# A hybrid decoder layer: order of copies, joins, chunks and the triangular solve in its front stage

## The chip, the cores and the metric

One NeuronCore of a Trainium2 chip runs the whole layer as one program. The metric is the device time of one execution in microseconds. The engines are TensorE (PE), VectorE (DVE), ScalarE (ACT), GpSimd (POOL) and SyncE (SP), which here issues the DMAs. Each engine runs its own list of instructions in order; semaphores make one wait for another.

## The reference, cut to what matters

For x of 1024 positions by 1024 columns: `h = RMSNorm(x)`; one projection `h @ w_in` gives an HGRN2 group (q, f, i, gate; four heads of 128) and a gated DeltaNet group (q, k, v through a causal convolution of width 4 with silu, z, and two gates per head).

```python
f = lb + (1.0 - lb) * jax.nn.sigmoid(hf)
o_a = hgrn2_chunked(silu(hq), 1.0 - f, hi, log(f))           # cumulative sum of log f in each chunk
qkv = silu(causal_dwconv(gqkv, gdn_conv)); gq, gk = l2_normalize(...)
system = eye + strict_lower((k * beta) @ k.T * exp(g_t - g_s)) # per chunk and head: its inverse is needed
attn = (q @ k.T) * exp(g_t - g_s)
```

Both groups are scanned over the chunks, gated, sent through `w_out` and added to x; then come a convolution-gated MLP (2816 wide) and a small embedding part. All of it is float32, with matmul operands split in a high part and a remainder (three matmuls for one product).

## The kernel before, in words

The order of work is written out by hand in `Front` (one method per engine). The kernel uses chunks of 128 positions, eight of them (NT = 8).

*Split products.* A weight slab is loaded into `w_raw`, rounded by ACT into `w_whi` (`Slabs.round`, L167; pieces L358), and DVE computes the remainder `w_wlo` (`Slabs.remainder`, L182; pieces L365). PE then does three matmuls for each of them.

*Conv pairs.* The 12 tiles of the DeltaNet q, k, v (128 columns each) are made in 6 pairs, each by seven products of half size in the Winograd form of Strassen's method: B21, T2, T3, T1, (B11 of the next pair), B22, T4, in `Pieces.order`. B11, T2, T1 and B22 of a pair accumulate one after the other in one PSUM bank, and between them ACT copies the bank out (`act_pair_copy`, L1060); PE opens the bank again only when that copy is done. DVE joins copies and banks into the convolution line (`dve_pair_join`, L1458), ACT copies B22 to the line (`act_pair_line`, L1072) and does the first tap (L1088), DVE the other three (`dve_taps`, L1468), ACT the silu (L1093). For the eight tiles of q and k come squares (ACT L1104, L1116; DVE remainder L1475) and a small matmul that sums them (`pe_sum`, L950). POOL forms the sums of weight blocks (L328 to L339). At the last pair ACT and DVE compute the decay factors (`act_factors`, `dve_factors`).

*Chunks and f units.* PE then computes eight units of f (head and half, `F_UNITS`), each 24 matmuls (L936 to L938), in 16 slots of 12. Between them it does the chunks: `pe_chunk` (transposed spreads L788, scores L793) in the second half of slot `SPREAD[c]` and `pe_chunk_turn` (transposes, L802) in the first half of the next. For each chunk DVE shifts (L1632), ACT takes exponentials (L1291, L1294) and scales the keys (L1299), DVE does four products (L1640 to L1649), and SP stores the tiles lt, at and kd (`sp_chunk`, L607). ACT applies the sigmoid to a finished f unit (L1242); each change between Sigmoid, Exp, Ln and Silu loads a table (ACT_TABLE_LOAD). `dve_open` (L1618, L1620) turns the sigmoid into f and 1 − f, `act_log` (L1283) takes the logarithm, `dve_cumulate` (L1610) the running sum, called a scan of f below.

*Solve.* Blocks of 32 × 32 of the stored lt are loaded back (`b_blk`), DVE inverts them in 31 steps of two operations (`dve_solve`, L1672, L1675), with slab remainders at given steps; POOL cuts x and its transpose xt out of it (L680, L683), SP stores them and loads them in scan form. Meanwhile PE does the f units and then eight units of q; in these lie the four steps of the first chunk's inverse (`INVERSE_AFTER`, L1861). Then the scan over the chunks starts (ACT L2045, L1272, L2036; DVE L2189), and later the output projection, the MLP and the embedding part.

SP's queue around the change is: reload of `saved`, per chunk the three stores with slab loads after chunks 1, 2 and 5, the blocks, lt, two slabs, then x stored, waited for and loaded, xt stored, waited for and loaded.

Of the kernel before, what the change touches and what calls it, by code (L numbers as in the profile page):

```python
# [54 lines left out]
class Kit:  # L55


    def __init__(self, nc, ctx):
        self.nc, self.ctx = nc, ctx
        self.psum = ctx.enter_context(nc.psum_tensor("psum", [P, 8, BANK], F32))  # L60
        c = lambda name, shape: ctx.enter_context(nc.sbuf_tensor(name, shape, F32))
        self.ident = c("ident", [P, P])
        self.ones = c("ones", [P, P])
        self.tri = c("tri", [P, P])
        self.future = c("future", [P, P])
        self.cols = c("cols", [P, N_COLS])
        self.eps = c("eps", [P, 2])
        self.lb = c("lb", [P, 2 * NH])

        self.spare = c("spare", [P, 2])  # L70
        with ExitStack() as early:
            w = lambda name: early.enter_context(nc.sbuf_tensor(name, [P, DM], F32R))
            self.more_hi, self.more_lo = ([w(f"w_more_{n}{u}") for u in range(2)] for n in ("hi", "lo"))
        with ExitStack() as rows:
            r = lambda name: rows.enter_context(nc.sbuf_tensor(name, [P, NH, BANK], F32))
            self.row_copy1, self.row_copy = r("row_copy1"), r("row_copy")
        with ExitStack() as pairs:
            r = lambda name, shape: pairs.enter_context(nc.sbuf_tensor(name, shape, F32))
            self.pair_line = [r(f"gconv_line{u}", [P, GK - 1 + SEQ]) for u in range(2)]
            self.pair_sum, self.pair_raw = r("pair_sum", [P, BANK]), r("pair_raw", [P, DM])  # L80
            self.gate_z = r("gate_z", [P, 10, NT, NH])
        with ExitStack() as blocks:
            r = lambda name, shape: blocks.enter_context(nc.sbuf_tensor(name, shape, F32))
            self.blk, self.xo, self.xto = (r("b_" + n, [P, SB, SB]) for n in ("blk", "x", "xt"))
            self.tmp = r("b_tmp", [P, SB * SB // 4])
        with ExitStack() as chunks:
            r = lambda name, shape: chunks.enter_context(nc.sbuf_tensor(name, shape, F32))
            r("a_more_before", [P, 2, SB, SB])
            self.more_lt, self.more_at = r("a_more_lt", [P, DG]), r("a_more_at", [P, DG])
        self.ed = [c(f"s_h_ed{i}", [P, DG]) for i in range(3)]  # L90
# [280 lines left out]
class Front:  # L371
# [6 lines left out]
    SPREAD = tuple(range(NT))  # L378
# [4 lines left out]
    INVERSE_AFTER = ((2, 1, 0), (3, 0, 0), (3, 0, 1), (3, 1, 1))  # L383
# [4 lines left out]
    def __init__(self, nc, k, a, shared, heads_on, rows_out, scratch, saved):  # L388
# [20 lines left out]
        with ExitStack() as chunks:  # L409
            self.dec = [s(f"a_dec{i}", [P, DG], c=chunks) for i in range(2)]  # L410
            self.egb, lt, at, self.kd = (s("a_" + n, [P, DG], c=chunks) for n in ("egb", "lt", "at", "kd"))
        self.lt, self.at = (lt, k.more_lt), (at, k.more_at)
# [26 lines left out]
        with ExitStack() as projecting:  # L439
# [5 lines left out]
        names = ("made", "loaded", "kept", "soft", "picked", "wrow", "squared", "rooted", "inverted", "scaled", "rounded_x",  # L445
                 "begun", "tapped", "freed", "smooth", "sq", "sq_hi", "sq_lo", "gate_in", "gate_hi", "gate_lo", "act", "dve",
                 "gated", "bounded", "logged", "summed", "ready", "shifted", "decayed", "queried", "lt_stored", "at_stored",
                 "kd_stored", "zeroed", "blocks", "solved", "cut", "x_stored", "opened", "formed", "sum_rounded", "sum_rest",
# [23 lines left out]
    def sp(self, sp):  # L472
# [68 lines left out]
        sp.wait_ge(s["lt_stored"], NT * 16)  # L541
# [10 lines left out]
        for n, (name, src) in enumerate((("x", self.xo), ("xt", self.xto))):  # L552
            sp.wait_ge(s["cut"], n + 1)
            for b in range(P // SB):
                at = slice(b * SB, (b + 1) * SB)
                sp.dma_start(self.scratch[name][at, :, at].rearrange("i g j -> g i j"), src[at, :, :]).then_inc(s["x_stored"], 16)
            sp.wait_ge(s["x_stored"], (n + 1) * (P // SB) * 16)
            self.scan.load_part(sp, name, 0, (self.scan.x, self.scan.xt[0])[n])
        for i in range(self.STAGES):
            sp.wait_ge(self.stored[i], 6 * 16)  # L560
        for name in ("at", "kd"):
            sp.wait_ge(s[name + "_stored"], NT * 16)
        for j in range(2):
            self.slabs.load(sp, first["q"] + NH + 1 + j)

# [37 lines left out]
    def sp_chunk(self, sp, c):  # L603
        part = slice(c * NH, (c + 1) * NH)
        for name, key, tile in (("lt", "a_kk", self.lt[c % 2]), ("at", "a_qk", self.at[c % 2]), ("kd", "a_k", self.kd)):
            self.banks.released(sp, (key, c))
            sp.dma_start(self.scratch[name][:, part, :], heads(tile[:])).then_inc(self.s[name + "_stored"], 16)  # L607
# [59 lines left out]
    def pool(self, pool):  # L667
# [14 lines left out]
        pool.wait_ge(s["at_stored"], NT * 16)  # L682
# [259 lines left out]
    def pe_sum(self, pe, m):  # L942
        at = self.place(m)
        pe.wait_ge(self.s["sq_lo"], at + 1)
        if at == 0:
            pe.wait_ge(self.s["picked"], 1)
# [171 lines left out]
    def act(self, act):  # L1118
# [35 lines left out]
        act.activation(self.pick[:], self.ones8[:], ACT.Copy).then_inc(s["picked"], 1)  # L1154
# [32 lines left out]
        for i, (p, q) in enumerate(pc.order):  # L1187
# [44 lines left out]
        for slot in range(self.SLOTS):  # L1232
# [3 lines left out]
            if slot == NT:  # L1236
                self.act_log(act, (0, 1))
            if slot % 2:
# [3 lines left out]
                self.banks.release(act.activation(self.f[:, h, half * BANK:(half + 1) * BANK], self.banks.of(key), ACT.Sigmoid), key)  # L1242
# [4 lines left out]
        self.act_log(act, (2, 3))  # L1247
        for name in ("lt", "at", "kd"):
            act.wait_ge(s[name + "_stored"], NT * 16)
        act.wait_ge(s["queried"], NT)  # L1250
        for h in range(NH - 1):
            for half in range(2):
# [3 lines left out]
                if half == 1:  # L1256
                    slabs.round(act, first["q"] + h + 2, m_)
        act.wait_ge(pc.made, pc.sums_made() + 1)
# [26 lines left out]
    def act_slot(self, act, slot):  # L1285
        s, small = self.s, self.small
        for c in range(NT):
            if self.SPREAD[c] == slot:
# [7 lines left out]
                if c:  # L1296
                    act.wait_ge(s["kd_stored"], c * 16)
                for h in range(NH):
                    ins = act.activation(heads(self.kd[:])[:, h, :], self.banks.of(("a_k", c))[:, h * P:(h + 1) * P], ACT.Copy,  # L1299
# [20 lines left out]
    def act_factors(self, act):  # L1320
        s, z, small, k = self.s, self.z, self.small, self.k
# [6 lines left out]
        act.sem_inc(s["act"], 1)  # L1328
        act.activation(z[:, 9], self.lnr[:, :, NH:2 * NH], ACT.Exp, scale=-0.5).then_inc(s["act"], 1)
# [5 lines left out]
        k.table(act, ACT.Silu)  # L1335
# [124 lines left out]
    def dve_taps(self, dve, m):  # L1460
        s, line, acc, at = self.s, self.line[m % 2], self.qkv[:, m, :], self.place(m)
        for q in range(1, GK):
            if q == 1:
                dve.wait_ge(s["begun"], at + 1)
            else:
                dve.wait_ge(s["tapped"], 2 * at + q - 1)
            tap = self.k.cols[:, C_GCONV + q * 3 * NH + m:C_GCONV + q * 3 * NH + m + 1]
# [9 lines left out]
    def dve(self, dve):  # L1477
# [68 lines left out]
        for i, (p, q) in enumerate(pc.order):  # L1546
# [29 lines left out]
            elif q == pc.T4:  # L1576
                self.dve_taps(dve, 2 * p + 1)
        self.dve_pair_join(dve, last, pc.T4)
        slabs.remainder(dve, self.first["f"] + 1)
        self.dve_taps(dve, 2 * last)  # L1580
        first = self.first
        for slot in range(NT):
            self.dve_slot(dve, slot)
            if slot in (5, 7):
                self.dve_open(dve, (slot - 5) // 2)
                slabs.remainder(dve, first["f"] + self.ROUNDED_AT[slot])
            if slot == 3:
                dve.memset(self.keep, 1.0).then_inc(s["ready"], 1)
                dve.wait_ge(s["ready"], 1)
                dve.memset(self.keep.rearrange("p (c t) -> p c t", t=P)[:, :, 0:1], 0.0).then_inc(s["ready"], 1)  # L1590
# [7 lines left out]
        dve.wait_ge(s["x_stored"], 2 * (P // SB) * 16)  # L1598
# [7 lines left out]
    def dve_cumulate(self, dve, h):  # L1606
        s = self.s
        dve.wait_ge(s["ready"], 2)
# [3 lines left out]
    def dve_open(self, dve, h):  # L1612

        s, k, f, kk = self.s, self.k, self.f[:, h, :], self.kk[:, h, :]
        for half in range(2):
            self.banks.released(dve, ("f", h, half))
        dve.wait_ge(s["kept"], 7)
# [4 lines left out]
    def dve_slot(self, dve, slot):  # L1622
        s, small, future = self.s, self.small, self.k.future
        for c in range(NT):
            if self.SPREAD[c] == slot:
# [11 lines left out]
                if c > 1:  # L1637
                    dve.wait_ge(s["lt_stored"], (c - 1) * 16)
                    dve.wait_ge(s["at_stored"], (c - 1) * 16)
# [11 lines left out]
    def dve_solve(self, dve):  # L1651
# [5 lines left out]
        for i in range(SB - 1):  # L1657
            if i == 9:
                slabs.remainder(dve, first["q"])
            elif i == 11:  # L1660
                self.dve_open(dve, 2)
            elif i == 17:
                self.dve_open(dve, 3)
# [76 lines left out]
class Scan:  # L1740
# [533 lines left out]
    def dve(self, dve):  # L2274
        s = self.s
        dve.wait_ge(self.front.s["summed"], NH)
        dve.wait_ge(self.front.s["x_stored"], 2 * (P // SB) * 16)
# [75 lines left out]
    def pool(self, pool):  # L2353
        pool.wait_ge(self.front.s["x_stored"], 2 * (P // SB) * 16)
# [1668 lines left out]
```

## Time and profile before

| | us |
|---|---|
| median of three runs | 1448.48 (1447.63 to 1450.18) |
| the profiled execution | 1446.5 |
| its span, first to last instruction | 1444.8 |
| PE busy | 1399.9 |
| DVE busy | 1098.4 |
| ACT busy | 753.7 |
| POOL busy | 287.2 |

The profile is of one execution. Busy shares are averages over stages; the windows split them, and the granted clock tells at which of its two levels (1.2 and 2.4 GHz) PE ran: 1.00 is always the upper one.

### The profile page before, as it was taken

What the parts mean: (1) busy time and instruction counts of PE and PEld (TensorE: products, weight loads), DVE (VectorE), ACT (ScalarE), POOL (GpSimd) and SP (SyncE); (2) the same over time, 40 slices, a digit from 0 to 9 for tenths busy, and PEclk for the clock granted to TensorE, in tenths of its full rate; (3) what the DMA queues carried; (4) which work ended last, traced back from release to release, by engine and by line L of the source; (5) the groups of instructions that cost most, each with busy time, mean ns of one, the idle gap of its engine ahead of it and who ended that gap; (6) DMA issues with size and microseconds to landing.
All of it is one profiled execution on the core that took longest, in us unless ns stands there. A gap on an engine that the chain in (4) does not pass through costs nothing.

```text
span 1444.8 us, 19770 instructions
## 1 busy us (share of the span) xinstructions
PE 1399.9 (97%) x7067; PEld 1171.0 (81%) x7067; DVE 1098.4 (76%) x1598; ACT 753.7 (52%) x1369; POOL 287.2 (20%) x279
## 2 busy tenths in 40 slices
PE   9999989877999999999999999999999999999998
PEld 7788866667788999888888888888888888888886
DVE  7843577755757988357997999999999686577567
ACT  6444455754437888347673434344444544454455
POOL 3251321111027877010000000000000154400000
PEclk9999999998999999999999999999999999999999
DMA  9715232245434333545442234335326765424213
GB/s 257 263 19 135 59 46 42 44 111 126 93 88 128 110 103 95 182 154 160 139 138 89 102 104 159 117 117 172 106 88 227 250 201 191 145 88 132 88 59 146
DMA packets 157345, 183.10 MB, mean 127 GB/s; under 512 B 21241, under 2 KB 96191, under 8 KB 157248
## 3 DMA queue, kind: packets, MB, share of 16 engines
q1 hardware_dynamic: 157248, 181.84, 42.3%
q8 instruction: 57, 0.93, 0.3%
q14 instruction: 40, 0.33, 0.1%
HBM read 130.43 MB, written 51.38 MB: 126 GB/s over the span
## 4 chain that ended last, share of the span: by engine, by line
PE 71%; DVE 5%; ACT 2%; issue 1%; DMA 1%; DVEq 0%; ACTq 0%
PE psum L2946 9%; PE psum L2947 9%; PE psum L2948 9%; PE psum L2887 5%; PE psum L2885 5%; PE psum L2886 5%; PE psum L1861 4%; PE psum L2860 4%; PE psum L2858 4%; PE psum L2859 4%; PE psum L1916 3%; PE psum L936 1%; PE psum L938 1%; PE psum L937 1%; PE psum L2843 1%
## 5 line engine op out<-in xcount | busy, mean ns | idle before, releaser
L3937 POOL TENSOR_TENSOR mixed_home<-mixed_home 128x512 f32<-128x512 f32 x11 | 14.8, 1349 | 507.8 <-DMA mixed_home<-in_w_down 503.8
L3679 DVE TENSOR_TENSOR g_slot<-w_raw,g_slot 128x512 fp32r<-128x512 f32 x77 | 71.4, 928 | 53.2 <-ACT g_slot L3253 53.1
L182 DVE TENSOR_TENSOR w_wlo<-w_raw,w_whi 128x1024 fp32r<-128x1024 f32 x42 | 58.1, 1384 | 66.8 <-ACT w_whi L167 66.7
L3253 ACT ACTIVATE g_slot<-w_raw 128x512 fp32r<-128x512 f32 x77 | 48.7, 632 | 104.8 <-PE psum L2887 99.7
L167 ACT ACTIVATE w_whi<-w_raw 128x1024 fp32r<-128x1024 f32 x42 | 44.4, 1060 | 89.4 <-PE psum L2860 78.4
L2858 PE MATMUL psum<-w_whi,m_hi 128*128 128x512 f32 x224 | 87.8, 392 | 0.0
L2860 PE MATMUL psum<-w_whi,m_lo 128*128 128x512 f32 x224 | 87.2, 389 | 0.0
L2859 PE MATMUL psum<-w_wlo,m_hi 128*128 128x512 f32 x224 | 87.2, 389 | 0.0
L2946 PE MATMUL psum<-m_hi,w_whi 128*128 128x512 f32 x212 | 82.8, 391 | 0.4 <-DVE w_wlo L2501 0.4
L2947 PE MATMUL psum<-m_lo,w_whi 128*128 128x512 f32 x212 | 82.5, 389 | 0.0
L2948 PE MATMUL psum<-m_hi,w_wlo 128*128 128x512 f32 x212 | 82.5, 389 | 0.0
L2946 PE MATMUL psum<-m_hi,w_more_hi 128*128 128x512 f32 x204 | 79.6, 390 | 0.0
L2948 PE MATMUL psum<-m_hi,w_more_lo 128*128 128x512 f32 x204 | 79.4, 389 | 0.0
L2947 PE MATMUL psum<-m_lo,w_more_hi 128*128 128x512 f32 x204 | 79.4, 389 | 0.0
L3357 ACT ACTIVATE pair_work<-pair_work,cols 128x1024 f32<-128x1024 f32 x18 | 20.8, 1157 | 109.3 <-DVE pair_work L3910 109.3
L2885 PE MATMUL psum<-w_more_hi,g_slot 128*128 128x512 f32 x156 | 60.8, 390 | 0.0
L2887 PE MATMUL psum<-w_more_hi,g_slot 128*128 128x512 f32 x156 | 60.7, 389 | 0.0
L2886 PE MATMUL psum<-w_more_lo,g_slot 128*128 128x512 f32 x156 | 60.7, 389 | 0.0
L2885 PE MATMUL psum<-w_whi,g_slot 128*128 128x512 f32 x152 | 59.2, 390 | 0.0
L2887 PE MATMUL psum<-w_whi,g_slot 128*128 128x512 f32 x152 | 59.1, 389 | 0.0
L2886 PE MATMUL psum<-w_wlo,g_slot 128*128 128x512 f32 x152 | 59.1, 389 | 0.0
L1468 DVE SCALAR_TENSOR_TENSOR qkv<-gconv_line,cols,qkv 128x1024 f32<-128x1024 f32 x36 | 53.1, 1474 | 5.1 <-ACT qkv L1088 4.2
(503 smaller groups left out, 4338.3 us busy)
## 6 DMA issues: line engine op xcount, KB each, us to landing
w_raw<-in_w_up SPq DMA_DIRECT2D x39, 512.0 KB, 3.9
s_rows<-pair_work SPq DMA_DIRECT2D x11, 1024.0 KB, 4.3
w_raw<-s_rows SPq DMA_DIRECT2D x44, 256.0 KB, 2.6
w_raw<-in_w_in SPq DMA_DIRECT2D x21, 512.0 KB, 9.1
g_rows<-pair_work SPq DMA_DIRECT2D x18, 512.0 KB, 2.6
w_raw<-g_rows SPq DMA_DIRECT2D x33, 256.0 KB, 3.1
w_raw<-in_w_out SPq DMA_DIRECT2D x16, 512.0 KB, 4.4
mixed_home<-in_w_down SPq DMA_DIRECT2D x32, 256.0 KB, 4.0
```

The source lines that it names most:

```text
L182: dve.tensor_tensor(lo[:], self.raw[j % self.RAW][:], hi[:].bitcast(F32), ALU.subtract).then_inc(self.rest, 1)
L1861: ins = pe.matmul(columns(self.hs(out, h)), left(h)[:, rows], columns(right(h)), start=True, stop=True)
L2858: pe.matmul(out, ah, wh, start=(kt == first), stop=False)
L2859: pe.matmul(out, ah, wl, start=False, stop=False)
L2860: ins = pe.matmul(out, al, wh, start=False, stop=(kt == last))
L2885: pe.matmul(out, slot[:, 0, part], wh, start=(i == 0), stop=False)
L2886: pe.matmul(out, slot[:, 0, part], wl, start=False, stop=False)
L2887: ins = pe.matmul(out, slot[:, 1, part], wh, start=False, stop=(i == self.KH - 1))
L2946: pe.matmul(out, wh[:, part], hi(kt), start=(start and kt == 0), stop=False)
L2947: pe.matmul(out, wh[:, part], lo(kt), start=False, stop=False)
L2948: ins = pe.matmul(out, wl[:, part], hi(kt), start=False, stop=(stop and kt == KT // 2 - 1))
L3679: dve.tensor_tensor(slot[:, 1, :], self.g_raw[u % 6], slot[:, 0, :].bitcast(F32), ALU.subtract).then_inc(self.s["split_lo"], 1)
```

## The change

- In the pairs, ACT copies T1's bank first and does the silu after it; the square follows the copy of B11.
- At the last pair, ACT does the logarithms where the factors were, and the exponentials after the loop; the first tap of tile 10 and the silu of tile 8 follow them, and the rounding of slab f+1 comes after these. DVE joins T4 between the second and the third of tile 11's taps, and does tile 10's taps ahead of the remainder of f+1.
- Each chunk is one slot later. In slots below 8 ACT copies f raw; at slot 8 it applies the sigmoid to heads 0 and 1 as a whole; the logarithms of heads 0, 1 come at slot 10, those of 2, 3 between q units.
- A second tile for the keys (`a_more_kd`), with a pair of semaphores for the stores of lt, at and kd each.
- DVE's four opens and four scans come after the slots and after the solve: open 0, 1, solve, open 2, 3, scans. Slab remainders in the solve stand at other steps.
- SP loads slab f+3 ahead of the chunks, and stores x and xt before it loads either. Two of the inverse's steps on PE are at other places.

```diff
-    SPREAD = tuple(range(NT))
+    SPREAD = tuple(range(1, NT + 1))
-    INVERSE_AFTER = ((2, 1, 0), (3, 0, 0), (3, 0, 1), (3, 1, 1))
+    INVERSE_AFTER = ((2, 1, 1), (3, 0, 0), (3, 0, 1), (3, 1, 0))
...
+        self.slabs.load(sp, first["f"] + 3)
         for c in range(NT):
             self.sp_chunk(sp, c)
-            if c in (1, 2, 5):
-                self.slabs.load(sp, first["f"] + {1: 3, 2: 4, 5: 5}[c])
+            if c in (2, 5):
+                self.slabs.load(sp, first["f"] + {2: 4, 5: 5}[c])
...
-                sp.dma_start(self.scratch[name]...).then_inc(s["x_stored"], 16)
-            sp.wait_ge(s["x_stored"], (n + 1) * (P // SB) * 16)
-            self.scan.load_part(sp, name, 0, (self.scan.x, self.scan.xt[0])[n])
+                sp.dma_start(self.scratch[name]...).then_inc(s[name + "_stored"], 16)
+        for n, (name, tile) in enumerate((("x", self.scan.x), ("xt", self.scan.xt[0]))):
+            sp.wait_ge(s[name + "_stored"], P // SB * 16)
+            self.scan.load_part(sp, name, 0, tile)
...
             pc.round(act, pc.ROWS + i + pc.AHEAD)
+            if before and before[1] == pc.T1 and 0 < before[0] < last:
+                self.act_silu(act, 2 * before[0] - 2)
             if before and before[1] == pc.B11:
                 self.act_pair_copy(act, before[0], pc.B11, self.y, pc.B21)
-            if before and before[1] == pc.T1 and 0 < before[0] < last:
-                self.act_square(act, 2 * before[0] - 2)
+                if q == pc.B22 and p:
+                    self.act_square(act, 2 * p - 2)
...
-            elif q == pc.T1 and 0 < p < last:
-                self.act_silu(act, 2 * p - 2)
             elif q == pc.B22 and p == last:
                 slabs.round(act, self.first["f"], m_)
-                self.act_factors(act)
-                self.act_silu(act, 2 * p - 2)
+                self.act_lens(act)
...
+        self.act_factors(act)
+        k.table(act, ACT.Silu)
+        self.act_tap(act, 2 * last)
+        self.act_silu(act, 2 * last - 2)
         m_.wait(act, ("pairs", last, pc.T4))
         slabs.round(act, self.first["f"] + 1, m_)
-        self.act_tap(act, 2 * last)
...
-            if slot == NT:
-                self.act_log(act, (0, 1))
             if slot % 2:
-                self.banks.release(act.activation(self.f[...], self.banks.of(key), ACT.Sigmoid), key)
-                if slot + 1 < NT:
-                    self.banks.released(act, key)
-                    k.table(act, ACT.Exp)
+                self.banks.release(act.activation(self.f[...], self.banks.of(key),
+                                                  ACT.Copy if slot < NT else ACT.Sigmoid), key)
+            if slot == NT:
+                for h in range(2):
+                    ...
+                    act.activation(self.f[:, h, :], self.f[:, h, :], ACT.Sigmoid).then_inc(s["soft"], 1)
+            if slot == NT + 2:
+                self.act_log(act, (0, 1))
...
-                if c:
-                    act.wait_ge(s["kd_stored"], c * 16)
+                if c > 1:
+                    act.wait_ge(s["kd" + self.STORED[c % 2]], c // 2 * 16)
...
-                self.dve_taps(dve, 2 * p + 1)
-        self.dve_pair_join(dve, last, pc.T4)
+                self.dve_taps(dve, 2 * p + 1, (lambda: self.dve_pair_join(dve, last, pc.T4)) if p == last else None)
+        self.dve_taps(dve, 2 * last)
         slabs.remainder(dve, self.first["f"] + 1)
-        self.dve_taps(dve, 2 * last)
-        for slot in range(NT):
+        for slot in range(NT + 1):
             self.dve_slot(dve, slot)
-            if slot in (5, 7):
-                self.dve_open(dve, (slot - 5) // 2)
-                slabs.remainder(dve, first["f"] + self.ROUNDED_AT[slot])
+            if slot in (6, 8):
+                slabs.remainder(dve, first["f"] + slot // 2 - 1)
...
-        self.dve_cumulate(dve, 0)
-        self.dve_cumulate(dve, 1)
+        self.dve_open(dve, 0)
+        self.dve_open(dve, 1)
         self.dve_solve(dve)
-        self.dve_cumulate(dve, 2)
-        slabs.remainder(dve, first["q"] + 3)
-        self.dve_cumulate(dve, 3)
+        self.dve_open(dve, 2)
+        self.dve_open(dve, 3)
+        for h in range(NH):
+            if h == 2:
+                slabs.remainder(dve, first["q"] + 3)
+            self.dve_cumulate(dve, h)
```

## Rows read from the trace of the kernel before

**Rows 1.** The page, part 1: busy us, share of the span, instructions.

```profile
PE 1399.9 (97%) x7067; PEld 1171.0 (81%) x7067; DVE 1098.4 (76%) x1598; ACT 753.7 (52%) x1369; POOL 287.2 (20%) x279
```

**Rows 2.** Windows: window, its length, busy us by engine, then PEclk, DMA share, GB/s.

```profile
180.00:292.00 112.00, 99.38 (x406) 75.35 (x405) 81.56 (x88) 67.07 (x96) 22.15 (x15) 0.92 0.28 44
...
292.00:373.00 81.00, 63.23 (x377) 55.29 (x375) 44.98 (x81) 42.92 (x78) 10.31 (x8) 0.89 0.56 129
...
320.00:330.00 10.00, 9.76 (x64) 8.38 (x63) 6.25 (x13) 3.84 (x10) 2.58 (x2) 1.00 1.01 61
```

**Rows 3.** PE's waits, 140 to 460 us: releaser, total, times, longest.

```profile
PE psum L920 <- ACT rows_stage L1060: 12.7, 5, 3.7
PE psum L802 <- ACT a_egb L1294: 6.5, 3, 3.6
PE psum L788 <- DVE gconv_line L1458: 4.9, 1, 4.9
PE psum L788 <- ACT a_kd L1299: 3.7, 1, 3.7
PE psum L936 <- DVE w_wlo L182: 3.2, 2, 2.7
PE psum L1861 <- ACT hgrn_q L1272: 1.6, 1, 1.6
```

**Rows 4.** Timeline of ACT, conv pairs: start, us, line, operation [idle before, releaser].

```profile
210.11 1.06 ACT L1093 ACTIVATE qkv<-qkv 128x1024 f32<-128x1024 f32 x1 [5.08 <-DVE qkv L1468]
211.08 0.58 ACT L1060 ACTIVATE rows_stage<-psum 128x512 f32<-128x512 f32 x1
...
216.33 0.60 ACT L1072 ACTIVATE gconv_line<-psum 128x512 f32<-128x512 f32 x1 [2.21 <-PE psum L923]
...
236.82 0.58 ACT L1060 ACTIVATE rows_stage<-psum 128x512 f32<-128x512 f32 x1
```

**Rows 5.** Timeline of DVE, conv pairs.

```profile
204.21 5.87 DVE L1468 SCALAR_TENSOR_TENSOR qkv<-gconv_line,cols,qkv 128x1024 f32<-128x1024 f32 x3
...
219.34 3.92 DVE L1468 SCALAR_TENSOR_TENSOR qkv<-gconv_line,cols,qkv 128x1024 f32<-128x1024 f32 x3
```

**Rows 6.** Timeline of PE, conv pairs: matmuls at the full clock.

```profile
207.66 0.39 PE L920 MATMUL psum<-h_hi,w_whi 128*128 128x512 f32 x1
...
208.34 0.39 PE L920 MATMUL psum<-h_hi,w_whi 128*128 128x512 f32 x1
```

**Rows 7.** Timeline of DVE, last pair.

```profile
295.13 3.92 DVE L1468 SCALAR_TENSOR_TENSOR qkv<-gconv_line,cols,qkv 128x1024 f32<-128x1024 f32 x3 [4.16 <-ACT qkv L1088]
```

**Rows 8.** Timeline of PE, chunk stage: two chunks' first transposes.

```profile
342.10 1.04 PE L788 MATMUL psum<-ident,gdn_small 128*128 128x128 f32 x8
...
348.39 0.82 PE L788 MATMUL psum<-ident,gdn_small 128*128 128x128 f32 x6
```

**Rows 9.** The chain in order of time (start, us), and ACT's timeline, chunk stage.

```profile
323.94 9.37 DMA kd_rows<-a_kd
...
370.28 1.28 ACT L1283 ACT_TABLE_LOAD   x1
371.58 2.01 ACT L1283 ACTIVATE hgrn_f<-hgrn_f 128x1024 f32<-128x1024 f32 x2
```

**Rows 10.** Timelines of SP, DVE and POOL around the solve.

```profile
365.94 0.32 SPq L607 DMA_DIRECT2D lt_rows<-a_more_lt  x1
...
377.34 0.09 DVE L1656 MEMSET b_blk<- 128x32 f32 x1
...
408.56 2.28 DVE L1610 TENSOR_TENSOR_SCAN hgrn_f<-hgrn_q,hgrn_f 128x1024 f32<-128x1024 f32 x1
...
408.78 3.13 POOL L680 TENSOR_SCALAR_AFFINE_SELECT b_x<-b_blk 128x1024 f32<-128x1024 f32 x1 [42.93 <-DVE b_blk L1675]
411.86 2.12 POOL L683 TENSOR_SCALAR_AFFINE_SELECT b_xt<-b_blk 128x1024 f32<-128x1024 f32 x1
```

**Rows 11.** Timeline of ACT at the scan's start.

```profile
439.22 1.95 ACT L2045 ACTIVATE s_h_ed<-s_h_ed 128x256 f32<-128x256 f32 x6 [3.73 <-DVE s_h_ed L2189]
```

More of the change, by code:

```diff
@@ L410, in __init__ @@
             self.dec = [s(f"a_dec{i}", [P, DG], c=chunks) for i in range(2)]
-            self.egb, lt, at, self.kd = (s("a_" + n, [P, DG], c=chunks) for n in ("egb", "lt", "at", "kd"))
-        self.lt, self.at = (lt, k.more_lt), (at, k.more_at)
+            self.egb, lt, at, kd = (s("a_" + n, [P, DG], c=chunks) for n in ("egb", "lt", "at", "kd"))
+        self.lt, self.at, self.kd = (lt, k.more_lt), (at, k.more_at), (kd, k.more_kd)
         with ExitStack() as mixed:
@@ L561, in sp, with all_stored, cut_stored @@
         for name in ("at", "kd"):
-            sp.wait_ge(s[name + "_stored"], NT * 16)
+            self.all_stored(sp, name)
         for j in range(2):
             self.slabs.load(sp, first["q"] + NH + 1 + j)
+    def all_stored(self, eng, name):
+        for which in self.STORED:
+            eng.wait_ge(self.s[name + which], NT // 2 * 16)
+    def cut_stored(self, eng):
+        for name in ("x", "xt"):
+            eng.wait_ge(self.s[name + "_stored"], P // SB * 16)
     def sp_values(self, sp, t):
@@ L604, in sp_chunk @@
         part = slice(c * NH, (c + 1) * NH)
-        for name, key, tile in (("lt", "a_kk", self.lt[c % 2]), ("at", "a_qk", self.at[c % 2]), ("kd", "a_k", self.kd)):
+        for name, key, tile in (("lt", "a_kk", self.lt[c % 2]), ("at", "a_qk", self.at[c % 2]), ("kd", "a_k", self.kd[c % 2])):
             self.banks.released(sp, (key, c))
-            sp.dma_start(self.scratch[name][:, part, :], heads(tile[:])).then_inc(self.s[name + "_stored"], 16)
+            sp.dma_start(self.scratch[name][:, part, :], heads(tile[:])).then_inc(self.s[name + self.STORED[c % 2]], 16)
     def pool_masks(self, pool):
@@ L1241, in act @@
                 m_.wait(act, key)
-                self.banks.release(act.activation(self.f[:, h, half * BANK:(half + 1) * BANK], self.banks.of(key), ACT.Sigmoid), key)
-                if slot + 1 < NT:
-                    self.banks.released(act, key)
-                    k.table(act, ACT.Exp)
+                self.banks.release(act.activation(self.f[:, h, half * BANK:(half + 1) * BANK], self.banks.of(key),
+                                                  ACT.Copy if slot < NT else ACT.Sigmoid), key)
+            if slot == NT:
+                for h in range(2):
+                    for half in range(2):
+                        self.banks.released(act, ("f", h, half))
+                    act.activation(self.f[:, h, :], self.f[:, h, :], ACT.Sigmoid).then_inc(s["soft"], 1)
+            if slot == NT + 2:
+                self.act_log(act, (0, 1))
         slabs.round(act, first["q"] + 1, m_)
-        self.act_log(act, (2, 3))
         for name in ("lt", "at", "kd"):
-            act.wait_ge(s[name + "_stored"], NT * 16)
+            self.all_stored(act, name)
         act.wait_ge(s["queried"], NT)
@@ L1257, in act @@
                     slabs.round(act, first["q"] + h + 2, m_)
+                if (h, half) == (1, 0):
+                    self.act_log(act, (2, 3))
         act.wait_ge(pc.made, pc.sums_made() + 1)
@@ L1318, in act_chain, with act_lens @@
         self.k.table(act, ACT.Silu)
[L1320 to L1321 removed]
+    def act_lens(self, act):
+        s, k = self.s, self.k
         self.multiplied.wait(act, "len_columns")
@@ L1328, in act_factors @@
         act.sem_inc(s["act"], 1)
+    def act_factors(self, act):
+        s, z, small = self.s, self.z, self.small
+        act.wait_ge(s["act"], 5)
         act.activation(z[:, 9], self.lnr[:, :, NH:2 * NH], ACT.Exp, scale=-0.5).then_inc(s["act"], 1)
@@ L1466, in dve_taps @@
                 dve.wait_ge(s["tapped"], 2 * at + q - 1)
+            if q == GK - 1 and before_last:
+                before_last()
             tap = self.k.cols[:, C_GCONV + q * 3 * NH + m:C_GCONV + q * 3 * NH + m + 1]
@@ L2276, in dve @@
         dve.wait_ge(self.front.s["summed"], NH)
-        dve.wait_ge(self.front.s["x_stored"], 2 * (P // SB) * 16)
+        self.front.cut_stored(dve)
         for lv in range(3, 6):
@@ L2353, in pool @@
     def pool(self, pool):
-        pool.wait_ge(self.front.s["x_stored"], 2 * (P // SB) * 16)
+        self.front.cut_stored(pool)
         for u in range(3):
```

46 lines of the change are left out of this document (23 added, 23 removed).

## The prediction

> **What bounds the kernel now.** I read the page's busy shares first: TensorE (PE) is busy 1399.9 of 1444.8 us [rows 1]. So nothing done on another engine shortens this kernel unless PE stands still for it, and the whole prize is PE's idle time plus what a halved clock costs it. Next the windows: from 180 to 373 us PE is not full [rows 2]. In the conv pairs (180 to 292) it idles 112 − 99.4 = 12.6 us, and the granted clock of 0.92 says that about 0.08 × 112 = 9 us more went to matmuls at 1.2 instead of 2.4 GHz; in the chunk stage (292 to 373) it idles 81 − 63.2 = 17.8 us and loses about 0.11 × 81 = 8.9 to the clock. PE's waits name the releasers [rows 3]: the pair copies (12.7), exponentials (6.5), the last join (4.9), the key copy (3.7), slab remainders (3.2), and at the scan's start hgrn_q (1.6). Only these 33 us and the clock behind them can be won: some 50 us, 3.5%.
>
> **Part 1, bank copy ahead of the silu.** B22 accumulates in the bank that T1 left, so PE waits for ScalarE's copy of T1. Before, ScalarE first waits 5.1 us for the taps, does the silu (210.11), then the copy (211.08); only then PE does B22, at 1.2 GHz, and the line copy waits for it until 216.33 [rows 4]; tap 1.05, rounding 0.55 and remainder 0.65 follow, and VectorE's next taps start at 219.34 [rows 5]. This is a loop: the taps of one tile end, ScalarE and PE work, the next taps begin. Its round is 236.82 − 211.08 = 25.7 us [rows 4]. PE's own work in it is 7 pieces of 12 matmuls, which start (208.34 − 207.66) / 3 = 0.227 us apart at the full clock [rows 6], 2.72 a piece, and two sums of 0.9: 20.8 us.
> After: T1 is copied when PE ends it, B22 follows without a pause, and PE leaves this half of the loop. What is left is ScalarE and VectorE. Taps end 210.1; VectorE does the T4 remainder (0.6), the square's remainder (1.2) and the join of B21 (0.6), until 212.45, and ScalarE's copy of B11 waits for that join, because both use one tile; copy 0.5, square 1.0, line 0.6, tap 1.1, rounding 0.5, remainder 0.65: next taps at 216.9 instead of 219.34. Gain 2.4 us a round, the round 23.3. PE's 20.8 doesn't set it: the missing 2.5 us come back as a new wait at the length sum ahead of T3, whose square remainder stands behind the taps on VectorE. The loop's other half (square, rounding, tap, copy of T2, remainder, taps) stays. Its taps take 5.87 us where the first half's take 3.92 [rows 5]; the pair sums on GpSimd lie beside them, start from the same remainders after as before, and so I keep 5.87.
> Three rounds (p = 1 to 3) give 7.2. In the round of p = 4 the decay chain's four table loads stand ahead of the copy, where they stay; the wait there was the longest (3.7, [rows 3]) and I count 2.0. Sum 9.2. Bounds: 4 (the B11 copy and the sum's wait eat half) and 21.6 (all idle and clock of the stage).
>
> **Part 2, last pair.** The exponentials of the factors move behind the last line copy and tap; VectorE's factors wait for them, and its taps of tile 11 queue behind. Tap 11 can end 290.9 (B22 ends 289.2, line 0.6, tap 1.1); a table load 1.28 and five small exponentials: 293.0, so the taps start there instead of at 295.13 [rows 7]. The join of T4 comes after two of three taps (2.6): 296.2 instead of 295.13 + 3.9 + 0.6 = 299.6. Taps of tile 11 end 297.5, of tile 10 (3.9) 301.4, and only then comes slab f+1's remainder (1.2): 302.6. Before it came ahead of tile 10's taps, at 300.8: that is this part's price.
>
> **Part 3, chunks one slot later, raw f, two key tiles.** Unhindered, a slot is 348.39 − 342.10 = 6.29 us of PE [rows 8]: chunk 2.6, turn 0.8, twelve f matmuls with hand-over 2.9. Two f slots (5.5) now come ahead of chunk 0, which starts at 292.0 + 5.5 = 297.5; its inputs (join 296.2, factors 293) are there, and the wait of 4.9 is gone. At 300.2 PE wants slab f+1 and waits 2.4. Then chunk 0's exponentials: shift ends 303.7, the table is there at 303.9, two exponentials 305.1, and PE asks at 304.0: 1.1. Before these were 4.9 and 2.65.
> From chunk 1 on, what broke the rhythm goes. The key copy waited for the store of the one key tile, 9.37 us [rows 9]; now it waits for the store of two chunks ago, 12.6 us earlier. The Sigmoid and Exp loads of 1.28 us around every f unit (8 loads) go. The bounds (1.5 us) that stood with a remainder in front of a shift go to the end; a remainder alone (1.2) fits into the 2.3 us between a turn and the next shift. Left is f+3's remainder behind chunk 7's last product: 0.6.
> PE from 292.0 to unit 5's first matmul: 5.5 + 8 × 6.29 = 55.8, plus 2.4, 1.1 and 0.6, plus 1.8 for the clock (8.9 over the five waits before, one such now): 61.7. Before 373.0 − 292.0 = 81.0. Gain 19.3. Bounds 10 (one store of 9.4 in front of a chunk's products) and 25.2 (81.0 − 55.8).
>
> **Part 4, solve first.** What PE needs later must also come some 20 us sooner. Chunk 7's last product falls to 349.8 (365.9 before, its store issued 365.94 [rows 10]). The solve began 377.34, 11.4 after it, behind two scans of 2.28; the blocks came between; I take 9, so 359 (361 at the latest). The sigmoids of f 0 and 1 (1.28 + 2 × 1.0) end 354.9, the two opens 357: hidden. Ten steps of the solve take 6.9, so q's remainder runs 366 to 367.6; PE wants it at 292 + 61.7 + 16.3 = 370: 2.4 to spare. The whole solve took 408.56 − 377.34 = 31.2; without two opens (3.0) and a wait of 2.1, some 27 with new small waits: 386. GpSimd's cuts take 3.1 and 2.1; with both stores queued ahead of the loads x is in its tile by 399, xt by 402; PE wants x at the end of q unit 5, near 402. VectorE: opens 3.0, scans 4 × 2.28, a remainder 1.2: 399.8, where before the cut's stores held it to 423. The Ln of tiles 2 and 3 sits between two silus (two more loads, 2.6) ahead of q+3's rounding, which VectorE meets at 394 without a wait.
> The small remainder wait (3.2 − 2.7 = 0.5, [rows 3]) goes. The last inverse step comes one piece, 2.7 us, earlier, so the exponentials of 439.22, which waited 3.73 [rows 11], and the q copy behind them come earlier: PE's 1.6 goes.
> On a table switch the row shows that the exponential begins 0.02 us after its load's end (load 370.28 to 371.56, [rows 9]). The Trainium skill (ScalarE: Activation LUTs, "What ACT_TABLE_LOAD costs") puts a switch at 1283 ns plus about 1380 ns of drain: the load agrees, the drain doesn't show. By the page the two new switches would cost 5.3 and the last scans end at 402.5, one us of wait for PE.
> On GpSimd: the cut beside a scan took 3.13, the scan 2.28 beside it and 2.2 alone, the second cut 2.12 [rows 10]. The Trainium skill (SBUF — State Buffer, "SBUF: two separate sides") says that a GpSimd operation and a VectorE one with two SBUF inputs exclude each other for the whole instruction. By it both cuts would queue with opens and scans, and x come about 2 us later, another us for PE.
>
> **Sum.** 9.2 + 19.3 + 0.5 + 1.6 = 30.6; I take off 1 for the margins under 3 us. The profiled execution (1446.5, span 1444.8) would take 1416.9; the median before is 2.0 above it, so 1418.9.
>
> **Rivals.**
> (a) *The stall moves.* PE waits at the sum, at B11's copy, at the late f+1, each time with a fall of the clock. For it: VectorE is busy 81.6 of 112 us in the pairs [rows 2], and the wait for f+1 is new. Against: these waits are counted. Pairs 4, chunks 13, rest 1: 18, so 1430. Chance 0.20.
> (b) *The solve doesn't follow.* PE stands for q's remainder or x. For it: margins of 1 to 3 us. Blocks 9 us late would cost 9 − 2.4 = 6.6: 1425; with x behind them too, 1433. Chance 0.06.
> (c) *The stores set the pace: slower.* A chunk stores three tiles of 256 KB in 6.3 us. At 320 to 330 us the DMA share was 1.01 at 61 GB/s [rows 2], and a store took 9.37. Were that the stores' own rate, a chunk would need 768/61 = 12.6 us, eight 101 against 73 before: +28 − 9 = +19, 1467. It decides above some 10 us a chunk (73 + 9 over eight). Against: over the whole stage the share was 0.56 at 129 GB/s; a slab load of small pieces fills the bad window. Chance 0.05.
> (d) *Not what it says.* The copy has another releaser than the silu, the loop stays and f+1's delay cancels the rest: within 0.2%, 0.03.
> The forecast with its own range, 1411 to 1425, has 0.62; better still (pairs at PE's rate, 6 to 9 us more, 1410) 0.04.
> 0.2% (2.9 us) is about what can be told from no change. Faster 0.92, same 0.03, slower 0.05. The range 1410 to 1436 holds the forecast, (a), (b).
>
> **What would show it.** Right: the copies out of T1's bank directly behind T1, no PE wait at B22 for p = 1 to 3 but 2 to 2.5 us at a length sum; 2 to 3 us for f+1 after chunk 0; chunks 6.3 us apart, none waiting for a key copy; the solve starting 18 us sooner after the last pair, no open between its steps; PE full from there to the scan. Wrong: new waits over 3 us in the q units, chunks over 8 us apart, stores above 10 us, or a change after 600 us.

## The result and the profile after

The changed kernel takes 1415.27 us (1415.08 to 1415.99), the kernel before 1448.06 beside it: ratio 0.9772, 95% interval 0.9755 to 0.9789, 32.8 us less. The predicted time was 1418.9. Of the two profiled executions (1446.5 and 1415.99) the span fell from 1444.8 to 1414.3, 30.5 us; the sum was 30.6 before its margin was taken off.

Page of the kernel after, part 1, against [rows 1]:

```profile
PE 1390.1 (98%) x7067; PEld 1163.5 (82%) x7067; DVE 1103.6 (78%) x1598; ACT 748.6 (53%) x1363; POOL 288.0 (20%) x279
```

PE does the same 7067 matmuls in 9.8 us less busy time: that part is the clock. Its idle time fell by 20.7 (1444.8 − 1399.9 = 44.9 to 1414.3 − 1390.1 = 24.2). The windows, cut where the same pieces end (columns as in [rows 2]; the first line is the kernel before, for the last stretch):

```profile
373.00:438.00 65.00, 64.43 (x304) 52.80 (x304) 40.94 (x81) 24.39 (x33) 12.49 (x11) 1.00 0.37 69
...
180.00:283.40 103.40, 94.46 (x407) 71.57 (x406) 81.47 (x86) 66.49 (x92) 22.25 (x15) 0.98 0.31 48
283.40:345.00 61.60, 57.80 (x378) 50.88 (x376) 42.54 (x78) 31.85 (x70) 10.28 (x8) 0.97 0.67 152
345.00:409.40 64.40, 64.39 (x304) 52.82 (x304) 49.59 (x89) 32.07 (x43) 12.11 (x11) 1.00 0.47 86
```

The pairs took 112 us and take 103.4; chunk stage 81.0 and 61.6; VectorE's busy time in them is the same within 0.1 (81.56) and lower by 2.4. The granted clock is 0.98 and 0.97 instead of 0.92 and 0.89. In the last window, f and q units up to the scan, PE stands still for 0.01 us (0.57 before): what the earlier stages gave is kept. PE's waits, 140 to 440 us, against [rows 3]:

```profile
PE psum L963 <- DVE len_sq_lo L1499: 3.8, 4, 1.1
PE psum L949 <- DVE w_wlo L184: 3.3, 2, 2.8
PE psum L933 <- ACT rows_stage L1073: 3.2, 2, 2.7
PE psum L933 <- DVE gconv_line L1480: 2.4, 3, 0.8
PE psum L1884 <- issue: 0.6, 1, 0.6
PE psum L815 <- ACT a_egb L1313: 0.5, 1, 0.5
```

33 us of waits became 14 us. L933 is L920 of before, L963 is L950, L949 is L936, L815 is L802, L1884 is L1861. The pair copies fell from 12.7 to 3.2, of which 2.7 is the one behind the decay chain; the exponentials fell from 6.5 to 0.5; the key copy, the last join in front of chunk 0 and hgrn_q are gone. The length sums grew to 3.8 (0.4 before), and the joins (2.4) are new. The slab remainders stayed at 3.3 in sum: the 2.7 in front of unit 5 became 0.5, 0.5 among the q units went, and the 2.75 for f+1 is new.

The pair loop on ScalarE and where PE now waits in it, against [rows 4]:

```profile
204.44 0.60 ACT L1073 ACTIVATE rows_stage<-psum 128x512 f32<-128x512 f32 x1 [1.46 <-PE psum L936]
...
208.07 1.06 ACT L1106 ACTIVATE qkv<-qkv 128x1024 f32<-128x1024 f32 x1 [2.52 <-DVE qkv L1492]
...
210.47 0.60 ACT L1073 ACTIVATE inverse_y<-psum 128x512 f32<-128x512 f32 x1 [0.81 <-DVE gconv_line L1480]
...
227.82 0.60 ACT L1073 ACTIVATE rows_stage<-psum 128x512 f32<-128x512 f32 x1 [1.48 <-PE psum L936]
```

```profile
211.72 0.47 PE L933 MATMUL psum<-h_hi,w_whi 128*128 128x512 f32 x1 [0.80 <-DVE gconv_line L1480]
...
221.21 0.40 PE L963 MATMUL psum<-len_sq_hi,len_pick 128*8 128x512 f32 x1 [1.07 <-DVE len_sq_lo L1499]
...
294.37 0.50 PE L949 MATMUL psum<-h_hi,w_whi 128*128 128x512 f32 x1 [2.75 <-DVE w_wlo L184]
...
296.93 0.88 PE L815 MATMUL psum<-ident,qkv 128*128 128x128 f32 x3 [0.52 <-ACT a_egb L1313]
```

The copy out of T1's bank now waits for PE (1.46), not for the silu, which comes 3.6 us after it. A round is 227.82 − 204.44 = 23.4 us. The copy of B11 waits for VectorE's join, as counted. Then come chunk 0's two waits, 2.75 for slab f+1 and 0.52 for the exponential (the view ends at 297.5, so that line has three of the eight transposes).

The solve, against [rows 10] (SP, DVE and POOL):

```profile
342.78 0.32 SPq L620 DMA_DIRECT2D lt_rows<-a_more_lt  x1
...
345.73 2.37 SPq L548 DMA_DIRECT2D b_blk<-lt_rows  x4
```

```profile
351.26 0.09 DVE L1683 MEMSET b_blk<- 128x32 f32 x1 [1.48 <-DMA b_blk<-lt_rows]
...
358.03 1.22 DVE L184 TENSOR_TENSOR w_wlo<-w_raw,w_whi 128x1024 fp32r<-128x1024 f32 x1
...
377.71 0.81 DVE L1645 TENSOR_SCALAR hgrn_f<-hgrn_f,lb 128x1024 f32<-128x1024 f32 x1
378.55 1.64 DVE L1647 TENSOR_SCALAR hgrn_k<-hgrn_f 128x1024 f32<-128x1024 f32 x1
380.11 2.60 DVE L1645 TENSOR_SCALAR hgrn_f<-hgrn_f,lb 128x1024 f32<-128x1024 f32 x1
```

```profile
377.92 1.72 POOL L693 TENSOR_SCALAR_AFFINE_SELECT b_x<-b_blk 128x1024 f32<-128x1024 f32 x1 [35.25 <-DVE b_blk L1698]
379.60 2.56 POOL L696 TENSOR_SCALAR_AFFINE_SELECT b_xt<-b_blk 128x1024 f32<-128x1024 f32 x1
```

It starts 8.5 us after the last lt store is issued, waits for nothing but its blocks, and lasts until open 2 begins, 377.71 − 351.26 = 26.5 us (31.2 before). From the end of the last pair piece to its start it is 67.8 us, 17.4 less than before (377.34 − 292.17 = 85.2); 18 had been forecast. The line at 358.03 is q's remainder.

### The profile page after: what moved, and what is told of

Read it like the earlier page. It is cut to its first block, busy times and chain, and to the rows that moved or that the text cites. A ratio compares the mean times of both kernels' runs of the same rounds, so it can differ in the third digit from the quotient of the medians.

```text
span 1414.3 us, 19775 instructions
## 1 busy us (share of the span) xinstructions
PE 1390.1 (98%) x7067; PEld 1163.5 (82%) x7067; DVE 1103.6 (78%) x1598; ACT 748.6 (53%) x1363; POOL 288.0 (20%) x279
## 4 chain that ended last, share of the span: by engine, by line
PE 89%; DVE 7%; ACT 2%; issue 2%; DMA 0%; DVEq 0%; ACTq 0%
PE psum L2969 9%; PE psum L2970 9%; PE psum L2971 9%; PE psum L2908 5%; PE psum L2910 5%; PE psum L2909 5%; PE psum L1884 5%; PE psum L2882 4%; PE psum L2883 4%; PE psum L2881 4%; PE psum L1939 3%; DVE qkv L1492 2%; PE psum L949 2%; PE psum L951 2%; PE psum L950 2%
## 5 line engine op out<-in xcount | busy, mean ns | idle before, releaser
L3380 ACT ACTIVATE pair_work<-pair_work,cols 128x1024 f32<-128x1024 f32 x18 | 20.8, 1156 | 109.2 <-DVE pair_work L3933 109.2
L2363 POOL TENSOR_TENSOR s_h_ql<-hgrn_q,s_h_ed 128x256 f32<-128x256 f32 x56 | 55.3, 989 | 3.5 <-ACT hgrn_q L1291 3.5
```

## The experiments

All times are medians; a ratio is to the kernel before on the same chip, and the kernel after has 0.9772 by the same measure. "Over after" is the difference of ratios times 1448. By the two ratios' 95% intervals it is good to about 3 us in copy_first_alone, silu_first_again, sigmoid_each and one_key, and to 4.5 to 6 us in the others, beside which the kernel before spread over some 9 us. The span of the profiled execution stands beside it, and PE's waits in the trace carry what is smaller. As a rough check of the times themselves: only one_key's four executions overlap with the 1415.08 to 1415.99 of the kernel after.

### Part 1 alone, and all but part 1

```diff
# copy_first_alone: the kernel before, with
+            if before and before[1] == pc.T1 and 0 < before[0] < last:
+                self.act_silu(act, 2 * before[0] - 2)
...
-            elif q == pc.T1 and 0 < p < last:
-                self.act_silu(act, 2 * p - 2)
# silu_first_again: the kernel after, with the same lines the other way
```

> The kernel before with the first part of the change alone: T1's bank is copied ahead of the silu, and the square follows B11's copy. Theory (the loop of taps, ScalarE and taps sets the pairs' pace, and PE leaves one half of it): each of three rounds gives 2.4 us, the fourth 2, in all 8 to 9.2 us, so about 1439.3. Rival (the wait only moves to B11's copy and the length sum, and half of it is lost): 4 us, 1444. Second rival (the part matters only together with the rest, as chunk 0 waits for the last join anyway): under 2 us.

Measured: 1439.08, ratio 0.9940 (0.9925 to 0.9954), 8.7 us less than before, span 1437.8. The theory held, at the place as well. The pair copies' wait fell from 12.7 us in five to 3.2 in two, and the sum and join waits (4.1 and 2.4) are those of the kernel after (3.8 and 2.4):

```profile
PE psum L950 <- DVE len_sq_lo L1475: 4.1, 5, 1.1
PE psum L920 <- ACT rows_stage L1060: 3.2, 2, 2.7
```

> The kernel after with the silu ahead of T1's copy again, as it was before. Theory: the loop's round grows from 23.3 to 25.7 us again, +8.6 us, about 1424. If the parts overlap (chunk stage and pairs share one cause), less than 5.

Measured: 1424.34, ratio 0.9835 (0.9821 to 0.9850), 9.1 over after, span 1424.3. Part 1 is worth the same alone and beside the rest (8.7 and 9.1), so within the noise they share nothing. PE's waits of this kernel, 140 to 450 us:

```profile
PE psum L933 <- ACT rows_stage L1073: 12.6, 5, 3.7
PE psum L949 <- DVE w_wlo L184: 3.3, 2, 2.8
```

### The table loads around the f units

```diff
# sigmoid_each: the kernel after, with
-                                                  ACT.Copy if slot < NT else ACT.Sigmoid), key)
-            if slot == NT:
-                ... (sigmoid over heads 0 and 1)
+                                                  ACT.Sigmoid), key)
+                if slot < NT:
+                    self.banks.released(act, key)
+                    k.table(act, ACT.Exp)
```

> The kernel after with the sigmoid on each f unit in slots 1, 3, 5, 7 again, a Sigmoid and an Exp table load around each, and no sigmoid over whole heads later. ScalarE's path between a key copy and the next exponential grows from 0.5 to 3.2 us, and there are about 2.3 us until the shifts are there: each of four slots loses up to 1 us on PE, +2 to +4. Rival (PE has 3.4 us of other work in that gap, so the loads are hidden): under 1 us, as the one wait of 0.24 us in such a slot before suggests.

Measured: 1419.73, ratio 0.9807 (0.9790 to 0.9823), 5.1 over after, span 1417.7 (3.4 more). The loads are not hidden: the wait for the exponential grew from 0.5 in one place to

```profile
PE psum L815 <- ACT a_egb L1310: 2.8, 4, 1.2
```

### One key tile, and the place of a slab load

```diff
# one_key: the kernel after, with
-        self.lt, self.at, self.kd = (lt, k.more_lt), (at, k.more_at), (kd, k.more_kd)
+        self.lt, self.at, self.kd = (lt, k.more_lt), (at, k.more_at), (kd, kd)
-                if c > 1:
-                    act.wait_ge(s["kd" + self.STORED[c % 2]], c // 2 * 16)
+                if c:
+                    act.wait_ge(s["kd" + self.STORED[(c - 1) % 2]], (c + 1) // 2 * 16)
# one_key_late_load: that, and
-        self.slabs.load(sp, first["f"] + 3)
...
-            if c in (2, 5):
+            if c in (1, 2, 5):
```

> The kernel after with one key tile: the key copy of a chunk waits for the store of the chunk before. Theory of the prediction: the key store that takes over 6 us stalls the chunks; the slab load after chunk 2 runs beside the stores of chunks 2 and 3, so one or two stalls of 2 to 4 us and a fall of the clock behind them: +3 to +6. Rival: with slab f+3 loaded before the chunks no store takes over 5 us any more, and one tile would do: under 1 us.

Measured: 1416.13, ratio 0.9779 (0.9765 to 0.9794), 1.0 over after by the ratio, span 1412.5, 1.8 less: no difference. The theory, that a store beside the slab load after chunk 2 would stall one tile, is refuted; the rival is right. So the next:

> One key tile, and slab f+3 loaded after chunk 1's stores again, as before the change (the run with one key tile and the early load lost nothing). Theory: it was the load's place that made a key store take 9.4 us, so now a key copy waits some 6 us for the store again and PE 3 to 4 with a fall of the clock: +4 to +6 us over after. Rival (the table loads around the f units set the phase in which the store was hit, and they are gone): under 1 us.

Measured: 1422.57, ratio 0.9818 (0.9792 to 0.9844), 6.7 over after, span 1420.8. ScalarE's waits, 280 to 350 us, of this kernel, of which the run with the early load has none for a store:

```profile
ACT a_kd L1317 <- DMA kd_rows<-a_kd: 6.4, 1, 6.4
```

the chain of waits in order of time (start, us), and the wait on PE that comes of it:

```profile
314.54 7.52 DMA kd_rows<-a_kd
```

```profile
PE psum L800 <- ACT a_kd L1317: 4.1, 1, 4.1
```

So with one key tile the place of f+3's load decides: with it after chunk 1, beside the load after chunk 2, a key store takes 7.5 us here and took 9.37 in [rows 9]; with it ahead of the chunks no key copy waits, and one tile does. Whether two tiles with the late load would do too was not tried, so it is not shown that the second tile alone would have failed.

### Slots, scans and inverse steps

```diff
# slots_back: the kernel after, with
-    SPREAD = tuple(range(1, NT + 1))
+    SPREAD = tuple(range(NT))
# scans_first: the kernel after, with
+        self.dve_cumulate(dve, 0)
+        self.dve_cumulate(dve, 1)
         self.dve_solve(dve)              # opens 2 and 3 in it again, at steps 11 and 17
...
# inverse_back: the kernel after, with
-    INVERSE_AFTER = ((2, 1, 1), (3, 0, 0), (3, 0, 1), (3, 1, 0))
+    INVERSE_AFTER = ((2, 1, 0), (3, 0, 0), (3, 0, 1), (3, 1, 1))
```

> The kernel after with the chunks in slots 0 to 7 again. Chunk 0's wait for the last join comes back at about 1.9 us, and its turn still waits for the shift behind tile 10's taps and f+1's remainder, at the same time as now (296.9); PE has done twelve f matmuls fewer by then. Theory: +2.2 to 2.7 us, the worth of one slot. Rival (the old 4.9 us wait comes back whole and its fall of the clock with it): +5 or more. Second rival (chunks earlier, solve earlier, nothing lost): 0.

Measured: 1420.6, ratio 0.9805 (0.9777 to 0.9833), 4.8 over after, span 1418.0 (3.7 more), against 2.2 to 2.7 expected. I had left out the clock. The turn's wait is longer, and the six f matmuls behind the turn ran at the lower level for 2.7 us (296.84 to 299.50), where they took 1.6 in the kernel after. PE's waits:

```profile
PE psum L815 <- ACT a_egb L1313: 4.6, 1, 4.6
...
PE psum L801 <- DVE gconv_line L1480: 1.9, 1, 1.9
```

> The kernel after with scans 0 and 1 ahead of the solve and opens 2 and 3 inside it, as before the change. Theory (the solve has 3 us of slack at q's remainder, no more): the solve starts 4.6 us late, q's remainder at step 10 comes 2.6 us too late for PE, and with the opens the next one another 2.9, so +5 to +6.5 us. Rival (the q units hide it, the order was free): under 1 us.

Measured: 1422.18, ratio 0.9815 (0.9788 to 0.9843), 6.2 over after, span 1422.3. The order was not free; the remainders in the solve were late twice:

```profile
PE psum L949 <- DVE w_wlo L184: 7.1, 4, 2.7
```

> The kernel after with the first chunk's inverse steps at their old places: the first a half q unit earlier, the last a half q unit later. Theory: the last exponentials come 2.7 us later again, behind them the copy of the last q unit, and PE waits 1.6 us at the solve of chunk 0: +1.5 to 2 us. Rival (the early first step waits for x, whose store ends later now): another 1 to 3 us on top. Second rival: 0.

Measured: 1417.57, ratio 0.9782 (0.9750 to 0.9813), 1.4 over after, span 1415.7 (1.4 more). The ratio alone doesn't tell 1.4 from nothing; the trace does, where the wait of [rows 3] is back:

```profile
PE psum L1884 <- ACT hgrn_q L1291: 1.6, 1, 1.6
```

### What bounds the loop and the last pair now

```diff
# square_later: the kernel after, with
                     self.act_silu(act, 2 * p - 1)
-                    self.act_square(act, 2 * p - 1)
...                                          # at T3, behind T2's copy and B22's rounding
                 if p:
+                    self.act_square(act, 2 * p - 1)
                     self.act_square_hi(act, 2 * p - 1)
# slab_first: the kernel after, with slab f+1 rounded ahead of act_tap(2 * last), and
+        slabs.remainder(dve, self.first["f"] + 1)
         self.dve_taps(dve, 2 * last)
-        slabs.remainder(dve, self.first["f"] + 1)
```

> The kernel after with the square of tile 2p-1 moved on ScalarE from behind its silu to behind the rounding of B22, ahead of its own rounding. Nothing else. If the loop of ScalarE and VectorE (23.3 us a round) is what PE waits for, the other half of the loop loses the 2.3 us that the square and its wait for the remainder take, the round falls to PE's own 20.8 to 21.2, and four rounds give 7 to 9 us: about 1407. Rival (PE itself or the length sums set the round, since its waits are at the sums): within 2 us of after.

Measured: 1409.35, ratio 0.9733 (0.9698 to 0.9767), 5.6 us under after, span 1407.9 (6.4 less); its slowest execution (1413.18) is below the fastest of the kernel after (1415.08). This is the step that shows the loop to be the bound: one square moved off it, no work taken away from any engine, and the round falls from 23.4 to 225.49 − 203.55 = 21.9 us on ScalarE's timeline, with T2's copies 21.9 and 21.4 apart:

```profile
197.12 0.58 ACT L1073 ACTIVATE rows_stage<-psum 128x512 f32<-128x512 f32 x1
203.55 0.60 ACT L1073 ACTIVATE rows_stage<-psum 128x512 f32<-128x512 f32 x1 [2.03 <-PE psum L936]
219.06 0.58 ACT L1073 ACTIVATE rows_stage<-psum 128x512 f32<-128x512 f32 x1
225.49 0.60 ACT L1073 ACTIVATE rows_stage<-psum 128x512 f32<-128x512 f32 x1 [2.03 <-PE psum L936]
240.49 0.57 ACT L1073 ACTIVATE rows_stage<-psum 128x512 f32<-128x512 f32 x1
```

The gain is less than the 7 to 9 us expected. The round stays above PE's 20.8, and sum waits of 3.1 us in all are left; what holds it there was not tried.

> The kernel after with slab f+1 rounded ahead of tile 10's tap and its remainder ahead of tile 10's taps. PE's wait of 2.75 us for it goes. Theory (VectorE's queue is what bounds this spot: tile 10's taps and chunk 0's shift come 1.2 us later, and PE then waits for them at the turn instead): the same wait, some 3 us, stands at the chunk's turn; within 1 us of after. Rival (the slab alone was late): −2.5 us.

Measured: 1418.17, ratio 0.9786 (0.9754 to 0.9817), 2.0 over after, span 1416.3 (2.0 more). The rival is refuted, and the theory held with a size too small: the slab is there in time, and all of the wait, and 1.6 more, stands at the turn:

```profile
PE psum L815 <- ACT a_egb L1313: 4.9, 1, 4.9
```

The chain in order of time (start, us) tells what the exponential waits for: behind the remainder come tile 10's three taps, the last of them at 292.91, then its silu and the load of the table for the exponentials.

```profile
289.22 1.14 DVE w_wlo L184
290.36 1.21 DVE qkv L1492
...
294.23 1.06 ACT qkv L1106
295.31 1.28 ACT L99
```

So the shift that the theory named with the taps is not the last link. In the kernel after the same chain (silu 293.21, table load 294.28) ends in the wait of 0.52, and the larger wait of 2.75 is not on it.

### Versions that beat both

```diff
# square_and_slab: square_later, slab_first, and
-    SPREAD = tuple(range(1, NT + 1))
+    SPREAD = tuple(range(2, NT + 2))
...                                          # q's remainders at steps 9 and 19 of the solve
# chain_in_two: square_and_slab, and
-                if p == last - 1:
-                    self.act_chain(act)
+                if p in (last - 2, last - 1):
+                    self.act_chain(act, p == last - 2)     # Exp and Ln part; then the sigmoid
```

> Meant to beat both: the square moved as in the run before (that gave 6 us), f+1's remainder first, chunks in slots 2 to 9, and q's remainders one and two steps earlier in the solve. PE does slot 2's f matmuls while VectorE does tile 10's taps. Theory: the waits of 2.75 and 0.56 fall to about 1.2, with the clock's share 2 to 3 us less than the run with the square alone, about 1406.5. Rival (the solve now comes too late for q's remainders, as chunks are a slot later and PE sooner): 1 to 3 us of new waits, so no gain over 1409.

Measured: 1406.9, ratio 0.9715 (0.9681 to 0.9750), span 1405.2, 2.7 less than with the square alone. f+1's wait is 1.4 instead of 2.7, and the exponential's 1.0 instead of 0.6. The ratios of the two runs alone don't tell them apart.

> The kernel of the run before with the decay chain's tables split over two rounds of the loop: the Exp and Ln part a round earlier, the sigmoid where it was, one more table load. Theory: the copy of T1 at p = 4 is then on time and PE's wait of 1.4 us there and its clock go: 1.5 to 2 us. Rival (ScalarE has no 4.4 us free in the round before, so the wait is only moved there): within 0.5.

Measured: 1406.31, ratio 0.9707 (0.9669 to 0.9745), span 1403.6, 1.6 less. In the times it can't be told from the run before; the copy's wait of 1.4 at p = 4 is gone from PE's waits, and the sums took 0.3 of it. It has the lowest median of all: 2.9% under the kernel before, 0.7% under the changed one. PE's waits, 140 to 450:

```profile
PE psum L963 <- DVE len_sq_lo L1502: 3.4, 5, 1.1
PE psum L949 <- DVE w_wlo L184: 1.4, 1, 1.4
PE psum L815 <- ACT a_egb L1313: 1.0, 1, 1.0
```

## Why the prediction was right

**Part 1** was sized at 9.2 us; PE's last pair piece ended 8.7 sooner (292.17 and 283.51), and the part alone is worth 8.7 by one run and 9.1 by the other. The round, 23.3 predicted, is 23.4. The step that named its limit (ScalarE's and VectorE's loop, not PE) is shown by square_later. A detail was missed: I put all of PE's new wait, 2.5 us, at the length sum, and it is 1.07 there and 0.80 at T4, which opens the bank that the join of T3 frees.

**Part 2** came as counted, shifted by the 8.7 of part 1: chunk 0 at 288.79 + 8.7 = 297.5 (297.5), f+1 at 302.8 (302.6) and the wait 2.75 (2.4), the exponential's wait 0.52 (1.1). The join of T4 ended 287.98 + 8.7 = 296.7 (296.2). This part was not undone by itself; in slots_back, where the chunks stand in their old slots, the wait for that join is 1.9 instead of 4.9.

**Part 3** took 61.6 us from the last pair to unit 5's first matmul (283.35 to 344.96; 61.7). But the reason given for one term is not borne out. I let the second key tile remove the key copy's 3.7 us and did not count the load of f+3 that now stands ahead of the chunks. one_key shows that tile to be worth nothing once that load is early, and one_key_late_load that with one tile the load's place is worth 6.7 us, 4.1 of them a wait of PE for the key copy. The change holds both, so the time came out right whichever of the two did it; if it was the load, that was luck, and the run that would tell (two tiles, late load) is missing. The chunks stand 6.3 us apart as counted (300.13 and 306.44), and none waits for a key copy. The table loads, which I had only counted as going, are worth 3.4 to 5.1 us (sigmoid_each).

**Part 4** had its first margin right: q's remainder ended 359.25, PE wanted it at 361.3, 2.0 to spare (2.4); and scans_first, which breaks that margin, costs 6.2 to 8. At the scan's start the wait of 1.6 for hgrn_q is gone, and putting it back cost 1.4 (inverse_back). The measured switch between tables is again without a drain: load 378.59 for 1.28, and after a wait for its data the logarithm; load 396.12, exponential 397.42, 0.02 us behind its end. (The row that the prediction reads for this, 371.58, is a logarithm too, L1283, and not an exponential; its gap is the same.)

The last scan ended 393.3, which is 402.0 on the prediction's clock, where it has 399.8. The delay is not a drain: beside the cuts two operations of the opens took 1.64 and 2.60 instead of 0.69 and 0.81, 2.7 us in all, and each ended 0.55 us after the cut that it overlapped (380.19 behind 379.64, 382.71 behind 382.16). These rows agree with the rule of the Trainium skill (SBUF — State Buffer, "SBUF: two separate sides") that whichever operation starts first holds the shared ports for its whole length. The opens have one tensor input, so by the page they fall under its case of a VectorE operation in a two-port mode, and not under the one of two SBUF inputs that the prediction names; no row here tells the mode. It cost PE nothing: PE stood still for 0.01 us in the whole stretch up to the scan.

**The rivals.** (a) was the wait moving: it did move, at the price in the sum and not at 18 us of gain. (b) had its condition 2.0 us away, and is what happens in scans_first. (c) was refuted: at 152 GB/s and a DMA share of 0.67 in the stage, no chunk waited for a store, and a key store landed in 2.3 us (median). (d) was refuted by copy_first_alone. The margin of 1 us that I took off wasn't needed. The median moved 2.3 more than the profiled executions did, and nothing in the mechanism accounts for that part.

## What to carry to other kernels

Where the bound engine is 97% busy, list its waits by releaser and add the clock they cost: that is the prize, and here the edits won some three fifths of it (30.5 of 50 us in the profiled executions). Find the loop that a wait belongs to and walk it in the new order, engine by engine; the shortest thing to move may be a square on another engine. When several edits go in at once, one that looks like the cure (a second buffer) can be idle beside one that removed the cause (a load out of the stores' way), and only undoing them one by one tells.

## What was not expected of the hardware

A wait of 4.6 us on PE cost another 1.1 us in the six f matmuls behind the turn (slots_back); one of 2.7 us cost 1.4 at 256.56 (12 matmuls in 4.1 instead of 2.7 us), and at 294.37 0.4 in six matmuls and 0.9 in the eight transposes behind them; the waits of about 1 us in the pairs left the granted clock of 180 to 240 us at 1.00, where before it was 0.93. On the shared ports both engines were held in turn. GpSimd's cut of x took 3.13 us in the kernel before and ended 1.07 us after the scan beside it (411.91 and 410.84); that scan was not slowed, 2.28 as alone [rows 10]. In the kernel after the same cut took 1.72 and ended 1.12 us after the open that was running when it began (379.64 and 378.52). So its own time seems to be about 1.1 us, an estimate from these two rows (GpSimd's spans in a profile are rough), and in both kernels it waited for the VectorE operation ahead of it, while the opens behind it waited for the cuts.
